# The ConvFFN of a hybrid layer: seven products from block 3 on, operand sums for the second column part on GpSimd, and a new order at the two borders and the end of the stage

## What is computed

```python
up = rms_norm(x, g_pre_ffn) @ w_up
buf = jnp.concatenate([conv_prev.astype(up.dtype), up], axis=1)
conv = b_conv + sum(w_conv[i] * buf[:, i:i + t] for i in range(CONV_WIDTH))
gate, val = jnp.split(conv, 2, axis=-1)
ff = (jax.nn.gelu(gate) * val) @ w_down
x = x + rms_norm(ff, g_post_ffn)
```

## Time and profile before

| | us |
|---|---|
| median of 3 runs (2183.42 to 2183.55) | 2183.55 |
| profiled execution, its own time | 2183.87 |
| its span | 2182.1 |
| this stage, from the release at 1407.1 to the end | 775 |
| of it up projection, to the last product's start at 1879.6 | 472.5 |

### The profile page before, as it was taken

One profiled execution on the slowest core, in us unless ns is written; L12 is line 12 of the kernel. 1 busy time (PEld: TensorE's weight loads), 2 busy tenths in 40 slices (PEclk: granted clock), 3 DMA queues, 4 the chain that ended last, 5 costly groups with the idle time before them and its releaser, 6 DMA issues. The chain is left out here.

```text
span 2182.1 us, 33718 instructions
## 1 busy us (share of the span) xinstructions
PE 2111.6 (97%) x13316; PEld 1997.8 (92%) x13316; DVE 1255.5 (58%) x1849; ACT 881.0 (40%) x1636; POOL 727.0 (33%) x453
## 2 busy tenths in 40 slices
PE   6999999999999999999999999999999999899997
PEld 6999999999899999998999978899999999788875
DVE  5036121000777888757656557597888788634565
ACT  4222201222777777755343122343433333323343
POOL 2325323443744444426565210003434343000000
PEclk9999999999999999999999999999999999899999
DMA  5124423555565555546666533311222222553654
GB/s 181 49 70 162 141 85 100 162 161 166 150 154 125 138 138 127 133 132 196 179 195 187 168 123 97 87 60 60 70 79 70 79 71 79 179 188 131 213 188 152
DMA packets 305651, 285.15 MB, mean 131 GB/s; under 512 B 51078, under 2 KB 270422, under 8 KB 305494
## 3 DMA queue, kind: packets, MB, share of 16 engines
q1 hardware_dynamic: 292576, 253.40, 40.1%
q10 hardware_dynamic: 10678, 21.47, 2.7%
q0 software_dynamic: 2240, 8.13, 1.0%
HBM read 203.59 MB, written 79.35 MB: 130 GB/s over the span
## 5 line engine op out<-in xcount | busy, mean ns | idle before, releaser
L294 PE MATMUL p_psB<-hT_lo,w_hi 128*128 128x364 f32 x888 | 295.6, 333 | 2.4 <-issue 2.4
L294 PE MATMUL p_psB<-hT_hi,w_lo 128*128 128x364 f32 x888 | 293.1, 330 | 0.0
L294 PE MATMUL p_psB<-hT_hi,w_hi 128*128 128x364 f32 x888 | 292.4, 329 | 0.0
L1185 DVE TENSOR_TENSOR_SCAN p_rest<-p_rest 128x896 f32<-128x896 f32 (+7 forms) x128 | 214.4, 1685 | 85.4 <-ACT p_rest L1108 85.4
L958 POOL TENSOR_TENSOR p_weights<-p_weights,p_rest 128x895 f32<-128x895 f32 (+7 forms) x128 | 160.3, 1258 | 208.0 <-DVE p_rest L1185 208.0
L582 ACT ACTIVATE p_line<-p_psB 128x364 f32<-128x364 f32 x108 | 51.3, 475 | 373.0 <-PE p_psB L294 373.0
L2689 DVE TENSOR_TENSOR p_w_lo<-p_w_raw,p_w_hi 128x512 fp32r<-128x512 f32 (+1 forms) x168 | 160.6, 961 | 57.2 <-ACT p_w_hi L2509 57.1
L294 PEld LDWEIGHTS p_psB<-hT_lo,w_hi 128*128 128x128 f32 x888 | 168.0, 189 | 3.2 <-issue 2.6
L294 PEld LDWEIGHTS p_psB<-hT_hi,w_hi 128*128 128x128 f32 x888 | 168.0, 189 | 0.0
L294 PEld LDWEIGHTS p_psB<-hT_hi,w_lo 128*128 128x128 f32 x888 | 167.7, 189 | 0.0
L2509 ACT ACTIVATE p_w_hi<-p_w_raw 128x512 fp32r<-128x512 f32 (+1 forms) x186 | 139.2, 772 | 60.2 <-DVE p_rows L2708 32.1
(11 more groups left out here) (371 smaller groups left out, 6082.3 us busy)
## 6 DMA issues: line engine op xcount, KB each, us to landing
p_w_raw<-in_w_down SPq DMA_DIRECT2D x66, 512.0 KB, 3.9
p_w_raw<-in_w_up SPq DMA_DIRECT2D x44, 512.0 KB, 5.0
w_raw<-in_w_in SPq DMA_DIRECT2D x40, 512.0 KB, 3.8
hid_scratch<-p_rows ACTq DMA_DIRECT2D x22, 545.0 KB, 2.8
p_kT<-k_hi_scratch SPq DMA_DIRECT2D x32, 256.0 KB, 4.5
p_kT<-k_lo_scratch SPq DMA_DIRECT2D x32, 256.0 KB, 5.3
w_raw<-in_w_gate SPq DMA_DIRECT2D x16, 512.0 KB, 4.6
p_raw_v<-in_cache_sb_v SPq DMA_DIRECT2D x8, 1024.0 KB, 6.1
```

The lines of the kernel that those rows point to most:

```text
L294: last = nc.tensor.matmul(out[:, 0:CH], stat[:, slot, w], mov[:, k, c], start=(at == 0), stop=(at == 3 * KT - 1))
L1185: nc.vector.tensor_tensor_scan(src, src, src, 1.0, ALU.mult, ALU.bypass).then_inc(s("scanned"), 1)
```

## The change

PLAIN goes from 4 to 3, so block 3 is done by seven products. The ten operations that build the sums T1 to T4 of the second column part, and the three that make their low parts (T1, T2, T4), go from DVE to the front of POOL's queue, with semaphores of their own (`t_raw_pool`, `t_lo_pool`). On DVE and ACT the weights of block 2 are split ahead of `convolve(1, 0)` and of `t_hi(2, 0)`. `store(PLAIN - 1)` comes after the two `p1` of the first fast block. `split_hi` and `split_lo` of the first two down passes go from behind the last block's gate convolution into the last block. The PSUM tables follow the shifted bank order. The last two passes of team 2 are done tile after tile, the squares in halves, each tile's root on its own; tile 7 is scaled by ACT, added by POOL and stored by ACT, tile 8 as before.

```diff
-    PLAIN = 4
+    PLAIN = 3
...
-    SIZE = [2 if key[0] == "down" else 1 for key in BUILDS]
+    ODD_END = (FT - 1, len(STEPS) - 1)
+    SIZE = [2 if key[0] == "down" or key == ODD_END else 1 for key in BUILDS]
...
-            ps = (ps_up[:, 0:2, :], ps_up[:, 2:4, :], psD[:, 0:2, :], psD[:, 2:4, :])[PAIR[m]]
+            ps = (psD[:, 2:4, :], ps_up[:, 0:2, :], ps_up[:, 2:4, :], psD[:, 0:2, :])[PAIR[m]]
...
+                chain = Chain(pool, s("pool_chain"))
...
+                def difference(out, spare, left, right):
+
+                    chain.step(nc.gpsimd.tensor_tensor(out, left[0], right[0], ALU.subtract))
+                    chain.step(nc.gpsimd.tensor_tensor(spare, left[1], right[1], ALU.subtract))
+                    nc.gpsimd.tensor_tensor(out, out, spare, ALU.add).then_inc(s("t_raw_pool"), 1)
...
+                difference(raised(1, 1), raised(1, 0), [part(p, 0, 1) for p in range(2)], [part(p, 0, 0) for p in range(2)])
+                pool.wait_ge(s("t_raw_pool"), 1)
+                remainder(2, 1, 1)
+                difference(t3[:, :, folded(1)], raised(4, 0), [part(p, 1, 1) for p in range(2)], [part(p, 0, 1) for p in range(2)])
+                pool.wait_ge(s("t_raw_pool"), 2)
+                remainder(4, 2, 0)
+                for which, high in ((2, 5), (4, 6), (1, 4)):
+                    T = {1: T1, 2: T2, 4: T4}[which]
+                    pool.wait_ge(s("t_hi"), high)
+                    nc.gpsimd.tensor_tensor(T[1][:, :, folded(1)], raised(which, 1), T[0][:, :, folded(1)].bitcast(F32),
+                                            ALU.subtract).then_inc(s("t_lo_pool"), 1)
                 for f in range(PLAIN, FT):
...
+                m = TEAMS[2][0]
+                pool.wait_ge(s("scaled"), 1)
+                pool.wait_ge(s("x2_ready2"), 16 * len(TEAMS[2]))
+                nc.gpsimd.tensor_tensor(x2[0:rows(m), m, :], acc_of(m), x2[0:rows(m), m, :], ALU.add).then_inc(s("finished_prompt"), 1)
...
-                    if q == 0 and step in ("S2", "S3"):
-                        pe.wait_ge(s("t_lo"), 2 + 3 * i if step == "S2" else 7 + i)
+                    if q == 0 and step == "S3":
+                        pe.wait_ge(s("t_lo"), 4 + i)
+                    elif q == 0 and i == 0 and step in ("S1", "S2", "A22"):
+                        pe.wait_ge(s("t_lo"), {"S1": 1, "S2": 2, "A22": 3}[step])
+                    elif q == 0 and step in ("S1", "S2", "A22"):
+                        pe.wait_ge(s("t_lo_pool"), {"S2": 1, "A22": 2, "S1": 3}[step])
...
+                for m in TEAMS[2]:
+                    for i in (len(PASSES) - 2, len(PASSES) - 1):
+                        down(i, (m,))
...
                     if f == 1:
                         t_hi(1, 0, 1)
+                        for j in range(4):
+                            weight_hi((f + 1, j))
                         t_hi(2, 0, 2)
                     if f == 2:
-                        t_hi(1, 1, 5)
-                    if f == 3:
-                        t_hi(4, 1, 8)
+                        t_hi(1, 1, 1)
+                        t_hi(2, 1, 2)
+                        t_hi(4, 1, 4)
...
-                    if f == PLAIN:
-                        store(f - 1)
                     p1(f, 0)
                     if f > PLAIN:
                         begin_gate(f - 1)
                     p1(f, 1)
                     high(0)
+                    if f == PLAIN:
+                        store(f - 1)
...
+                    if f == FT - 1:
+                        split_hi(0)
+                        split_hi(1)
                     high(5)
...
-                split_hi(0)
-                split_hi(1)
                 gelu(FT - 1)
...
+                act.wait_ge(s("half_rooted"), 1)
+                act.wait_ge(s("half_evac"), 2)
+                nc.scalar.activation(acc_of(m), acc_of(m), ACT.Copy, scale=rstd[0:rows(m), m:m + 1]).then_inc(s("scaled"), 1)
+                act.wait_ge(s("finished_prompt"), 1)
+                act.dma_start(o["y_prompt"][0, m * P:(m + 1) * P, :], x2[0:rows(m), m, :]).then_inc(s("stored"), 16)
```

More of the change, by code:

```diff
@@ L2366, in _ @@
                         sp.dma_start(x2[0:rows(m), m, :], d.x2[m * P:m * P + rows(m), :]).then_inc(s(f"x2_ready{team_of(m)}"), 16)
[L2367 to L2371, removed]
+                sp.wait_ge(s("finished"), TILES - 1)
+                sp.dma_start(o["y_sample"][0], x2[0:rows(TILES - 1), TILES - 1, :]).then_inc(s("stored_sample"), 16)
+                sp.wait_ge(s("stored_sample"), 16)
             @block.gpsimd
@@ L2440, in product, with down @@
                     last.then_inc(s("prod"), 1)
-                def down(i):
+                def down(i, team):
                     g, f = PASSES[i]
@@ L2475, in turn_tails @@
                     for j in range(4):
-                        last = nc.tensor.transpose(psD[0:2 * FT, 2, j * P:(j + 1) * P], tails[:, j, :], ident[:, :])
+                        last = nc.tensor.transpose(psD[0:2 * FT, 0, j * P:(j + 1) * P], tails[:, j, :], ident[:, :])
                     last.then_inc(s("tails_turned"), 1)
@@ L2581, in square, with square_half @@
                     act.wait_ge(s("squares"), m + 1)
+                def square_half(m, h):
+                    r, n = rows(m), 2 * TEAMS[2].index(m) + h
+                    if h == 0:
+                        act.wait_ge(s("left_done"), TEAMS[2].index(m) + 1)
+                    else:
+                        act.wait_ge(s("done"), m + 1)
+                    if n >= 2:
+                        act.wait_ge(s("half_squares"), n - 1)
+                    w = slice(h * HALF, (h + 1) * HALF)
+                    nc.scalar.activation(junk[0:r, w], pair(m)[0:r, w], ACT.Square, accum_out=half_ss[0:r, n:n + 1]).then_inc(s("half_squares"), 1)
                 for n in range(2):
@@ L2895, in _ @@
                 convolve(FT - 1, 0)
-                split_lo(0)
-                split_lo(1)
                 weight_lo(("down", 3))
@@ L2915, in _ @@
                 for m in TEAMS[2]:
-                    evacuate(m)
-                normalise(2)
-                for m in TEAMS[2]:
-                    finish(m)
+                    begin_root(m)
+                    evacuate_half(m, 0)
+                    evacuate_half(m, 1)
+                    root_of(m)
+                m = TEAMS[2][1]
+                dve.wait_ge(s("x2_ready2"), 16 * len(TEAMS[2]))
+                dve.wait_ge(s("half_evac"), 2 * len(TEAMS[2]))
+                nc.vector.scalar_tensor_tensor(out=x2[0:rows(m), m, :], in0=acc_of(m), scalar=rstd[0:rows(m), m:m + 1],
+                                               in1=x2[0:rows(m), m, :], op0=ALU.mult, op1=ALU.add).then_inc(s("finished"), 1)
 _INS = ["x_prompt", "x_sample", "cache_sb_k", "cache_sb_v", "state_ffn_conv", "g_pre_mix", "w_in", "ln_v_g", "ln_v_b",
```

83 lines of the change are left out of this document (56 added, 27 removed).

## The result

The changed kernel takes **2195.15 us** (median of 5 runs, 2193.64 to 2196.46), the kernel before, in the same session, 2183.55 (2183.42 to 2186.32): ratio 1.0049, 95% interval 1.0037 to 1.0061. The forecast was 2196. The profiled execution has a span of 2192.4 us against 2182.1.

A forecast was written before the change was run, and what follows sets the result against it. PE, busy 97% of the span, bounds the kernel in general, with the DVE and ACT loop setting the fast blocks' pace. Up projection +18.6, border -6.5, end 0: +12.1 us on 2183.87, so 2196 us, range 2185 to 2204.

The forecast's parts named there:

- The turns: Blocks 0 to 2: DVE and POOL hold each other off a whole instruction; POOL's 13 operations cost 33.0 us.
- The up projection's end: End of the up projection: store of block 4 at 1550.7 instead of 1532.1, so +18.6 us.
- my walk: DVE's queue followed from 1407.1 with turn prices: `store(2)` about 1503.7, first fast block's store at 1529.1.
- The reading of PE there: PE waits for weights at block 2 (about 5 to 9 us), S2 of block 3 (4 to 7), `v` (3.7).
- a rival's: Rival (c): border gives nothing, or low clock slows blocks 2 and 3 as well: +18.6, 2202 us; 13%.
- "The place of the first stores decides when the up projection ends": Fast blocks: the loop over DVE and ACT sets 21.59 us per store; PE, which was ahead, is caught up.
- up to 4.9: First fast block: without moving `store(PLAIN - 1)` the sum would be more by this many us (3.2 wait, 1.7 clock).
- some 1.7 us of it ran at the lower: Early fast blocks, kernel before: mean clock 0.91 read as 1.7 us at 1.2 instead of 2.4 GHz.
- The rival (b): Up projection: side engines catch up at 21.0 us a block, PE's own work binds: +2.3, 2186 us; 10%.
- Border: Border to the down projection: lost 6.1 instead of 9.9 + 2.7 us, so -6.5 us (-4.8 to -8.2).
- End: After the last matmul: POOL's addition holds tile 8's root on DVE, so 0 (bounds -2.2 and 0).
- The sum: Whole kernel: 18.6 - 6.5 + 0 = +12.1 us on 2183.87, giving 2196 us.

The follow-up runs named there:

- filled: Changed kernel with POOL's ten sums replaced by six fills that read nothing, low parts still on POOL: 2180.01 us, ratio 0.9981.
- weights_first: Changed kernel with POOL's three sums of block 3's weights ahead of the three low parts of T in its queue: 2194.32 us, ratio 1.0048.
- lows_late: Changed kernel with block 2's four low parts on DVE back behind block 1's gate convolution and T3 and T4: 2198.50 us, ratio 1.0067.
- store_first: Changed kernel with the last plain block's store back ahead of block 3's two `p1`: 2195.87 us, ratio 1.0053.
- dve_sums: Changed kernel with the same thirteen sums and low parts on DVE instead of POOL: 2178.15 us, ratio 0.9973.
- loop_before: Kernel before, with next block's first high part ahead of the gate's begin (ACT) and low part ahead of the gate convolution (DVE): 2181.28 us, ratio 0.9987.
- loop_after: Changed kernel, POOL's sums kept, with the fast blocks' loop shortened by moving next block's first high and low parts earlier: 2187.24 us, ratio 1.0012.
- borders_only: Kernel before (four plain blocks, sums on DVE) with only the store's move, the early first two splits and the halved end: 2178.38 us, ratio 0.9974.
- dve_loop_end: Changed kernel with the thirteen sums and low parts on DVE, the shorter fast-block loop and tile 7's end on DVE: 2168.19 us, ratio 0.9934.

## Why the prediction was right, and where it was not

- **The turns** (one instruction each, also for tiny copies) are as read from the two rows of the kernel before, and filled shows that they are the cause. Their price was too high: I added the whole durations, 2.54 + 0.6 and 2.54 + 1.2. Measured are 2.94 and 3.4. That instructions in a row take less than their sum is seen on DVE alone as well: four low parts of 0.69 take 2.50. So gelu(0) came at 1430.6 instead of 1432.4, the product of block 0 ended at 1439.1 instead of 1441.7, the weight sums of block 3 ended at 1484.3 instead of 1487.5, and `store(2)` came at 1499.95 instead of 1503.7.
- **The up projection's end**: +18.6 forecast, +15.2 in the profiles' own times (+15.7 counted from the phase's start). The difference is `store(2)`'s; the first fast block's store came 25.4 us behind it as in my walk, and the rest 21.6 apart.
- **The reading of PE there** was poorer than the number. I had PE wait at block 2 and at S2 of block 3 and named a wait for `v` of 3.7; measured 6.0, 5.2 and 1.2, and a wait of 2.8 at A11 of block 3 that I didn't name. The low clock behind these waits (0.83, 0.91, 0.83 of three stretches, where the kernel before has 1.00) I had only as a rival's. The sum still held, since the walk over DVE, the store, ACT and POOL gives `store(2)`, and the time follows the stores: against the changed kernel, the first fast block's store comes 0.1, 2.8 and 1.8 us later from the phase's start in weights_first, lows_late and store_first and 14.1 and 16.1 earlier in filled and dve_sums, and A changes by 0.0, +2.8, +1.8, -14.4 and -16.5, though PE's waits at blocks 2 and 3 differ widely.
- **"The place of the first stores decides when the up projection ends"** holds for the changed kernel, where PE has no lead left. For the kernel before it is wrong by the lead: 7.6 us earlier stores gave 2.4 us (loop_before). It was wrong also in what it promised of the store's move, "up to 4.9": 1.8 us on A (store_first), 0.6 in the kernel before, 3.3 there with the shorter loop. And "some 1.7 us of it ran at the lower" level misreads 0.91: at half the speed a stretch of 20 us with this mean has over 3 us at that level; 1.7 is about what they cost, and so the sum uses it.
- **The rival (b)**, side engines that catch up at 21.0 us a block, had 2186. They don't, by themselves; with the edit that lets them, loop_after has 2187.2. Its price was about right (A +10.0 for +8.8) and its condition not met.
- **Border**: -6.5 forecast, -5.3 measured. The two waits are 1.85 and 2.12 for 2.0 and 2.4; the clock is 0.83 in 1900 to 1920, which costs 3.4 us of the 20, where I took 1.7. In borders_only, with the same border, it is 0.91 (1880 to 1900), and the border gives 6.8. Which of the two comes after a wait is not given by its length: one of 3.5 us at block 3 is followed by 0.91 in dve_sums and by 0.83 in dve_loop_end, the one of 2.2 at block 2 by 1.00 before and 0.91 in borders_only. So this term was a guess within its bounds, and it stays open what decides it.
- **End**: 0 forecast, +0.4 measured. The held one-column step was forecast; its exact cost is 2.0 us, which eats what the halves give.
- **The sum**: +15.7 - 5.3 + 0.4 = +10.8 against +12.1; the ratio gives +10.7 (8.1 to 13.3). That 2196 lies within 1 us of the median is in part luck: the late stores were put 3.4 us too late and border and end together 1.6 too good, and the median stands 0.9 above the profiled execution's 2194.2, where I had put it 0.3 below.

What stays open too: the spread of the phase's start, 10 us between profiles of the same code ahead of it, whose cause lies outside this change.

## What to carry to other kernels

Work moved from DVE to POOL is not work taken away from DVE, as long as both read two operands from SBUF: the length of POOL's instruction is DVE's waiting time, and POOL's is twice DVE's for the same sum (2.53 and 1.29 us here). Two rows of a profile in which both are at work tell this ahead of time. And before an edit in a loop is priced by the loop's period, see in the count of matmuls by stretch from when on the loop holds PE. Until then a faster loop gives nothing; and where it holds PE in the end, time that PE gains ahead of it is mostly lost again.

## What the runs showed of the hardware

- A POOL instruction that only writes (a fill, 1.01 us for 1,088 elements) doesn't hold off DVE's low parts of 512 elements (2.50 us for four, filled). One that reads holds DVE off until its end, be DVE's instruction two elements long (2.30 us for 0.16) or 1,090 (7.24 for two of 2.75 together).
- A DVE operation with one operand in PSUM goes on beside POOL. DVE and POOL in a fast block of the changed kernel:

```profile
1613.31 1.29 DVE L2755 TENSOR_TENSOR p_w_lo<-p_w_raw,p_w_hi 128x512 fp32r<-128x512 f32 x1
1614.53 0.78 DVE L2850 TENSOR_TENSOR p_rows<-ps_up,p_snap 128x272 f32<-128x272 f32 x2
```

```profile
1612.76 1.30 POOL L2421 TENSOR_TENSOR p_w_raw<-p_w_raw 128x512 f32<-128x512 f32 x1 [4.04 <-DVE p_w_lo L2755]
1614.02 1.74 POOL L2424 TENSOR_TENSOR p_w_lo<-p_w_raw,p_w_hi 128x512 fp32r<-128x512 f32 x1
```

  The low part, 0.69 alone, stands until POOL's first ends; the two additions from PSUM take their 0.39 each within POOL's second. In a fast block much of DVE's work reads PSUM, in blocks 0 to 2 none of it does: this may be why the fast blocks bear POOL's weight sums; no run tests it.
- A turn takes 0.2 to 0.3 us less than the two durations together: 2.94 us for 2.54 and 0.6, 3.4 for 2.54 and 1.2. Why, no run shows.
